# Attention output products placed inside the HGRN turns, token-wise norm roots, and an eight-tile first part of the expert values

## What is computed

```python
# HGRN2, per head, in chunks of tokens; then norm and gate
A = einsum('bthd,btshd,bshd->bhts', qc, decay, kc)
o = einsum('bhts,bshv->bthv', A, vc) + einsum('bthd,bhdv->bthv', qc * exp(b), S)
S = exp(bl)[..., None] * S + einsum('bshd,bshv->bhdv', kc * exp(bl[:, None] - b), vc)
o = rmsnorm(o, g_hgrn) * silu(hg)
# merge: each mixer's output is projected to 1024 channels and gated by channel
mix = sigmoid(za) * (attn @ w_a) + sigmoid(zb) * (o @ w_b)
x = x + mix @ w_out
# experts: every token takes a few of 16,384; e runs over a token's experts
x = x + sum_e gate[e] * gelu(h @ u[e]) * v[e]
```

## Time and profile before

| | us |
|---|---|
| median of 3 runs | 2248.57 (2244.8 to 2250.56) |
| profiled run | 2249.61 |
| its span | 2248.0 |
| PE busy | 2088.7 (93%) |
| DVE busy | 1338.3 (60%) |
| POOL busy | 555.1 (25%) |
| ACT busy | 360.5 (16%) |
| mean granted clock of TensorE | 0.943 |

### The profile page before, as it was taken

The page is one execution under the profiler, slowest core; times in us unless marked ns, Lnnn a source line. Parts: engine busy times, 40 slices in busy tenths (PEclk is TensorE's granted clock), DMA queues, the critical chain, the costliest instruction groups (busy, mean ns, idle before and its releaser), DMA issues. The chain is left out here.

```text
span 2248.0 us, 24729 instructions
## 1 busy us (share of the span) xinstructions
PE 2088.7 (93%) x8839; PEld 1568.6 (70%) x8839; DVE 1338.3 (60%) x2881; ACT 360.5 (16%) x745; POOL 555.1 (25%) x516
## 2 busy tenths in 40 slices
PE   6968989976999999899999999999699999999997
PEld 4755577753889966677777777777477777777776
DVE  2005377763454158599999999988635455455233
ACT  1001137641010111211111222221000000000011
POOL 1001100013000000233335555554434244343000
PEclk9988999987559999999999999999899999999998
DMA  3142221113232332487889999999999999999421
GB/s 131 38 68 76 75 94 50 45 37 114 94 133 81 113 113 94 162 298 274 291 324 362 403 402 396 399 401 408 399 381 339 376 369 383 387 353 356 181 80 62
DMA packets 168033, 513.81 MB, mean 229 GB/s; under 512 B 18422, under 2 KB 52862, under 8 KB 164327
## 3 DMA queue, kind: packets, MB, share of 16 engines
q1 hardware_dynamic: 93782, 273.61, 33.6%
q0 software_dynamic: 60288, 213.96, 24.9%
q10 hardware_dynamic: 13840, 24.66, 2.9%
HBM read 462.42 MB, written 49.74 MB: 228 GB/s over the span
## 5 line engine op out<-in xcount | busy, mean ns | idle before, releaser
L1938 PE MATMUL ex_ps<-proj,ex_ring 128*128 128x320 f32 x2048 | 558.3, 436 | 20.5 <-DMA ex_ring<-in_v 20.5
L1883 PE MATMUL ex_ps<-h,ex_ring 128*128 128x320 f32 x2048 | 566.0, 433 | 5.9 <-DMA ex_ring<-in_uT 5.9
L1938 PEld LDWEIGHTS ex_ps<-proj,ex_ring 128*128 128x128 f32 x2048 | 392.4, 192 | 186.0 <-DMA ex_ring<-in_v 21.7
L1883 PEld LDWEIGHTS ex_ps<-h,ex_ring 128*128 128x128 f32 x2048 | 384.2, 191 | 156.6 <-DMA ex_ring<-in_uT 6.1
L2114 DVE TENSOR_TENSOR proj<-proj 128x320 f32<-128x320 f32 x124 | 53.0, 490 | 253.9 <-DMA proj<-scratch_a 234.4
L2048 DVE SCALAR_TENSOR_TENSOR gx_sum<-proj,gx_sum 128x1024 f32<-128x1024 f32 x120 | 154.2, 1285 | 9.2 <-DVE gx_sum L2048 0.9
L2030 DVE CUSTOM_DVE_ANT_0 proj<-proj,gx_tokens 128x1024 f32<-128x1024 f32 x120 | 143.9, 1222 | 2.1 <-DMA proj<-in_u,at_last 1.8
L1785 POOL DMA_INDIRECT scores<-in_u,at_last x26 | 30.9, 1187 | 435.6 <-POOLq L1504 389.1
L1791 POOL DMA_INDIRECT proj<-in_v,at_last x76 | 105.3, 1386 | 84.0 <-DVE gx_sum L2048 68.2
L379 PE MATMUL gate_ps<-h,work 128*128 128x260 f32 x512 | 120.5, 389 | 3.4 <-DMA work<-in_w_t 3.4
L1785 POOL DMA_INDIRECT proj<-in_u,at_last x76 | 88.2, 1161 | 141.9 <-DVE proj L2030 129.5
(11 more groups left out here) (387 smaller groups left out, 2743.1 us busy)
## 6 DMA issues: line engine op xcount, KB each, us to landing
ex_ring<-in_uT SPq DMA_DIRECT2D x128, 512.0 KB, 6.7
ex_ring<-in_v SPq DMA_DIRECT2D x128, 512.0 KB, 6.9
scratch_a<-ex_gelu ACTq DMA_DIRECT2D x64, 320.0 KB, 7.1
scratch_w<-proj SPq DMA_DIRECT2D x10, 2048.0 KB, 12.0
proj<-scratch_a SPq DMA_DIRECT2D x15, 1280.0 KB, 10.0
proj<-scratch_w SPq DMA_DIRECT2D x15, 1280.0 KB, 11.2
work<-in_w_t SPq DMA_DIRECT2D x37, 512.0 KB, 3.6
mg_ring<-in_w_q SPq DMA_DIRECT2D x32, 512.0 KB, 3.4
```

The lines of the kernel that those rows point to most:

```text
L1883: last = nc.tensor.matmul(y[:, bank(n), 0:TD], u[:, n % UR, k, :], xn[:, k, 0:TD], start=(k == 0), stop=(k == DC - 1))
L1938: last = nc.tensor.matmul(y[:, m, 0:TD], ring[:, (E1 + e) % UR, m * P:(m + 1) * P], hidden_of(part_of[e])[:, e - parts[part_of[e]][0], :], ...
```

## The change

**HGRN and merge.** The 64 attention products move out of `merge_tail` into `hgrn`, as sixteen half products (`att_product(i)`: one of eight output tiles m, one half of 260 tokens, four products each). Each turn holds four: after the scores, after the second chunk of kv, in the middle of `out` (at h == 2), and after `sample_out(2t)`. Each waits for its weights (even i) and for the gate of the one before (`s_eg`), since all share one half bank. DVE's `gate_att(i)` multiplies in place into `proj` (ZA). The weights (eight loads of 256 KB on ACT's queue, between the rows of v) take two of the four `spare` buffers, so the rows of v have two left. `out(t)` has one bank now, and waits for the copy of out(t - 1). In `merge_tail` only the second half of w_ab is loaded; the norm's sums are made token-wise, as twenty one-column products into one bank, so one root and one reciprocal of 128x20 do for all heads, and PE spreads them again over partitions by products with the identity (four of 128 columns and one of 8 for each head). DVE reads the spread root from PSUM, and `mix` is the sum of `proj` (ZA) and the gated HGRN product.

```diff
+        wa = [t.rearrange("p (k n) -> p k n", k=4) for t in spare[2:4]]
+        vb = spare[0:2]
+        WR = len(wa)
+        per_turn = DC * 2 // NT
...
+                def att_product(i):
+                    m = i // 2
+                    if i % 2 == 0:
+                        pe.wait_ge(s_wa[m % WR], 16 * (m // WR + 1))
+                    if i >= 1:
+                        pe.wait_ge(s_eg, i)
+                    o, c0, c1 = att_at(i)
+                    for k in range(4):
+                        last = nc.tensor.matmul(o, wa[m % WR][:, k, :], attT[:, k, c0:c1], start=(k == 0), stop=(k == 3))
+                    last.then_inc(s_ea, 1)
...
                     pe.wait_ge(s_st, (4 * t + 3) * HG)
-                    if t >= 2:
-                        pe.wait_ge(s_oc, t - 1)
+                    if t >= 1:
+                        pe.wait_ge(s_oc, t)
                     for h in range(HG):
-                        o = pO[:, t % 2, h * P:(h + 1) * P]
+                        if h == HG // 2:
+                            att_product(t * per_turn + 2)
+                        o = pO[:, 0, h * P:(h + 1) * P]
...
                 for t in range(NT):
+                    i = t * per_turn
                     scores(t)
+                    att_product(i)
                     for j in range(P // CH):
                         kv_of(t * (P // CH) + j)
+                        if j == 1:
+                            att_product(i + 1)
                     if t >= 1:
                         sample_out(2 * t - 1)
                     out(t)
                     sample_out(2 * t)
+                    att_product(i + 3)
...
+                def gate_att(i):
+                    dve.wait_ge(s_ea, i + 1)
+                    o, c0, c1 = att_at(i)
+                    gate = proj[:, ZA + i // 2, c0:c1]
+                    nc.vector.tensor_tensor(gate, o, gate, ALU.mult).then_inc(s_eg, 1)
...
+                load_weights(0)
+                load_weights(1)
+                act.wait_ge(s_vd, 16)
+                load_row(0)
+                load_row(1)
+                for t in range(1, NT):
+                    load_weights(2 * t)
+                    load_row(2 * t)
+                    load_row(2 * t + 1)
+                    load_weights(2 * t + 1)
...
+            act.wait_ge(s_ms, 1)
+            nc.scalar.activation(tiny[:, 0, :], ps[:, 7, 0:HG * (NT + 1)], ACT.Sqrt, scale=1.0 / P,
+                                 bias=c.eps[:, 0:1]).then_inc(s_rt, 1)
...
-                if hd >= 2:
-                    pe.wait_ge(s_rt, hd - 1)
-                for j in range(2):
-                    last = nc.tensor.matmul(ps[:, 4 + 2 * (hd % 2) + j, 0:HALF], c.ones[:, :],
-                                            sq[:, hd, j * HALF:(j + 1) * HALF], start=True, stop=True)
-                last.then_inc(s_ms, 1)
-            for m in range(DC):
-                if m % 2 == 0:
-                    pe.wait_ge(s_ab[m // 2], 16)
-                if m >= 2:
-                    pe.wait_ge(s_ga, m - 1)
-                for j in range(2):
-                    for k in range(4):
-                        last = nc.tensor.matmul(ps[:, 2 * (m % 2) + j, 0:HALF], ab[:, m, k, :],
-                                                attT[:, k, j * HALF:(j + 1) * HALF], start=(k == 0), stop=(k == 3))
-                last.then_inc(s_p, 1)
+                for t, n0 in enumerate(starts):
+                    i = hd * (NT + 1) + t
+                    last = nc.tensor.matmul(ps[:, 7, i:i + 1], sq[:, hd, n0:n0 + P], c.ones[:, 0:1], start=True, stop=True)
+            last.then_inc(s_ms, 1)
+            pe.wait_ge(s_iv, 1)
+            for hd in range(HG):
+                out = root_of(hd)
+                for t in range(NT + 1):
+                    col = tiny[:, 1, hd * (NT + 1) + t:hd * (NT + 1) + t + 1].to_broadcast([P, P])
+                    if t < NT:
+                        nc.tensor.matmul(out[:, t * P:(t + 1) * P], col, c.ident[:, :], start=True, stop=True)
+                    else:
+                        last = nc.tensor.matmul(out[:, TP:N], col, c.ident[:, P - TS:P], start=True, stop=True)
+                last.then_inc(s_sp, 1)
...
-            pe.wait_ge(s_n, 4 * HG)
+            pe.wait_ge(s_n, 3 * HG)
...
-                dve.wait_ge(s_rt, hd + 1)
-                link(nc.vector.reciprocal(rt[:, hd, :], rt[:, hd, :]))
+                dve.wait_ge(s_sp, hd + 1)
                 link(nc.vector.scalar_tensor_tensor(out=hgoT[:, hd, :], in0=hgoT[:, hd, :],
-                                                    scalar=c.small["g_hgrn"][:, 0:1], in1=rt[:, hd, :],
+                                                    scalar=c.small["g_hgrn"][:, 0:1], in1=root_of(hd)[:, 0:N],
                                                     op0=ALU.mult, op1=ALU.mult))
                 link(nc.vector.tensor_tensor(hgoT[:, hd, :], hgoT[:, hd, :], proj[:, HGT + hd, :], ALU.mult))
...
+            dve.wait_ge(s_rt, 1)
+            nc.vector.reciprocal(tiny[:, 1, :], tiny[:, 0, :]).then_inc(s_iv, 1)
+            for hd in range(HG):
                 norm(hd)
-                gate_att(2 * hd - 2)
-                gate_att(2 * hd - 1)
-            for hd in range(HG):
                 dve.wait_ge(s_sg, hd + 1)
                 link(nc.vector.tensor_tensor(hgoT[:, hd, :], hgoT[:, hd, :], sg[:, hd, :], ALU.mult))
-            gate_att(DC - 2)
-            gate_att(DC - 1)
```

```diff
-    HEAD = 4
+    HEAD = 8
+    QUAD = 4
...
-                return small[:, HEAD * TD:HEAD * TD + LATE * HEAD * WB].rearrange("p (k e n) -> p k e n", k=LATE, e=HEAD)
+                t = M.S_full[0].rearrange("p g k -> p (g k)")
+                return t[:, 0:LATE * HEAD * WB].rearrange("p (k e n) -> p k e n", k=LATE, e=HEAD)
...
-            for r in range(2):
-                sp.wait_ge(s_as[r], 16 * (E1 // 4))
-            for r in range(2):
-                sp.wait_ge(s_ws[r], 16 * (NWB // 2))
-            sp.wait_ge(s_h, HEAD)
-            load_hidden(1)
-            load_weights(1)
-            load_weights(2)
             for e in range(E1):
                 if e + UR < E1:
                     sp.wait_ge(s_pv, e + 1)
                     load_v(e + UR)
+                if e == 2:
+                    for r in range(2):
+                        sp.wait_ge(s_as[r], 16 * (E1 // 4))
+                        sp.wait_ge(s_ws[r], 16 * (NWB // 2))
+                    sp.wait_ge(s_h, HEAD)
+                    load_weights(1)
+                    load_hidden(1)
+                    load_weights(2)
...
+                if (quad + 1) * QUAD < HEAD:
+                    continue
+                while chunk < U_CHUNKS + (NC - U_CHUNKS) * (quad + 1) // (E1 // QUAD):
```

More of the change, by code:

```diff
@@ L994, in hgrn, with att_at @@
         s_m = a.sem("hg_zero_state")
-        VR = len(spare)
+        s_wa = [a.sem(f"hg_att_weights_loaded{r}") for r in range(WR)]
+        s_ea, s_eg = (a.sem("hg_" + x) for x in ("att_product", "att_gated"))
+        def att_at(i):
+            j = i % 2
+            return pO[:, 1, 0:HALF], j * HALF, (j + 1) * HALF
+        VR = len(vb)
         s_vd = a.sem("hg_v_rows_stored")
@@ L1099, in _ @@
                     ins.then_inc(s_sc, 1)
+                    i = t * per_turn
+                    gate_att(i)
                     for j in range(P // CH):
@@ L1117, in _, with load_weights, load_row @@
                 dve.wait_ge(s_oc, NT + 1)
+                dve.wait_ge(s_eg, DC * 2)
             @block.scalar
             def _(act):
[L1121 to L1123 removed]
+                def load_weights(m):
+                    if m >= WR:
+                        act.wait_ge(s_ea, 2 * (m - WR + 1))
+                    act.dma_start(wa[m % WR], I["w_ab"][m, :, 0:4, :]).then_inc(s_wa[m % WR], 16)
+                def load_row(b):
                     if b >= VR:
                         act.wait_ge(s_vc, b - VR + 1)
[L1126 removed]
+                    act.dma_start(vb[b % VR], v_dram[b:b + 1, :].to_broadcast([P, HG * P])).then_inc(s_vl[b % VR], 16)
+                act.dma_start(v_dram, hitok[0:TS, NT, :]).then_inc(s_vd, 16)
+                load_weights(0)
[8 more added lines that the diff above has]
+                    load_weights(2 * t + 1)
             @block.sync
@@ L1305, in merge_tail, with root_of @@
         a = Alloc(nc, ctx)
-        ab = M.S_all[:, 0:DC * DC * P].rearrange("p (m c n) -> p m c n", m=DC, c=DC)
+        wb = M.S_all[:, 0:DC * 4 * P].rearrange("p (m c n) -> p m c n", m=DC, c=4)
         mix, tb = M.mix, a.sb("mg_b", [P, 2, TD])
         ps = a.ps("mg_ps", [P, DC, 512])
-        s_ab = [a.sem(f"mg_weights_loaded{i}") for i in range(4)]
-        s_p, s_q, s_ga, s_gb, s_m = (a.sem("mg_" + k) for k in (
-            "att_product", "hgrn_product", "att_gated", "hgrn_gated", "mixed"))
+        s_wb = [a.sem(f"mg_weights_loaded{i}") for i in range(4)]
+        s_q, s_gb, s_m = (a.sem("mg_" + k) for k in ("hgrn_product", "hgrn_gated", "mixed"))
```

(26 more changed lines are left out.)

34 lines of the change are left out of this document (11 added, 23 removed).

## The result

The changed kernel takes 2254.43 us (median of 14 runs, 2251.0 to 2260.77) against 2248.32 us (14 runs) before: ratio 1.0029, 95% interval 1.0022 to 1.0037. By the medians that is 6.1 us slower. The profiled execution of the changed kernel took 2260.77 us, the longest of its 14, so 6 us of what its trace shows are its own; the first experiment says where they lie.

The account below looks back on a forecast made before the run. TensorE, busy for 93% of the span, was taken as the bound, with a low clock in HGRN and stalls in v. 2249.6 + 20 - 12 - 0.4 = 2257.2, less 1.0, gave 2256 us, own range 2247 to 2265.

Parts of the forecast that it names:

- its own yardstick of 6.7 us: Whole kernel: about 0.3%, what a measurement tells from no change; "same" runs from 2242 to 2255 us.
- HGRN, +20: HGRN: sixteen added half products at a changing clock, +17.5, and a weights' wait, +2.5; range -9 to +59 us.
- the clock's rise: HGRN: dense products across each turn's seam lift the clock at the scores' end; a turn takes 24.9 us.
- The terms that I put at nothing: HGRN: waits for DVE's gates, for the single bank of out and for broadcast rows in two buffers, each 0 us.
- Rival A: HGRN: the clock never rises, +59 us, with merge -9: 2298 us; chance 0.07.
- rival B: HGRN: the clock stays up throughout, -9 us, with merge -19: 2220 us; chance 0.10.
- Merge, -12: Merge tail: first HGRN product 14.2 us earlier, with 2 us given back for slower products.
- v, -0.4: v part: later start 5.8 and waits of 5 and 7 us against old stalls of 18.2; range -15.3 to +12.
- the 9 us of tile 7: v part: upper bound of the wait for tile 7, with loads landing in 25.5 us; 5 was taken.
- the 12 of tile 13: v part: upper bound of the wait for tile 13, with a tile's median 6.9 us after 21.5; 7 was taken.
- the -9 of HGRN at 1.00: HGRN: lower bound of its term, all products at the upper clock, 72 us of work and "10 less".
- Rival C: v part: waits for tiles 7 and 13 vanish, only a later start of 2.9 us is left, 2241 us; chance 0.16.

Follow-up runs that it names:

- the first experiment: Two kernels, each with one half of the change, the rest as before: HGRN and merge alone 2250.63 us (ratio 1.0007), experts alone 2252.02 us (1.0014).
- the evenly spread kernel: Changed kernel with the same 64 products, alternating banks and sixteen spread over each turn without a dense run: 2286.36 us, ratio 1.0176 to before.
- the second table: Changed kernel with the same 64 products, alternating banks, a dense start and a more careful spread of places: 2236.03 us, ratio 0.9957 to before.

## Why the prediction was right

It said 2256 and slower by a little, for these reasons; 2254.4 was measured. By its own yardstick of 6.7 us the 6.1 us lie at the upper edge of "same"; with 14 runs of each kernel the interval, 1.0022 to 1.0037, is clear of no change. That the sum came within 2 us is in part luck: by the means of the traces HGRN cost 6 us less than forecast (+14 for +20), while v and the u part cost +4.2 where -0.4 stood.

**HGRN, +20: right in kind, near in size, with the clock's rise at the wrong place.** +18.2 in the profiled execution, +14 in the mean of four traces. The weights' wait is 2.62 us where I had worked out 2.5, and the mean clock 0.71 where I had said near 0.7. The terms that I put at nothing held: for the gates, the one bank and the rows in two buffers PE waits 0.29 us in all. The clock goes up and down as I had said, and three of its four falls lie in `out`. The step that failed is the rise: I put it at the end of the scores behind each seam, and three of five rises came in `out`, behind its half product, while the first turn had none until there and stayed at 0.50 for 27.65 us. The two errors have opposite signs, so the length of a turn came out better than its picture. I had also not seen that the changes come at other places from one execution to the next (first rise at 600.1 in one trace, at 580.3 in another), with 92.6 to 101.6 us for the same code; what decides between them isn't shown. Rival A, 57 us from a clock that stays low, came true for three turns of four in the evenly spread kernel, and rival B in the second table: both were states of the same products; between the two kernels their order made the difference, though within the even spread one order stood at both levels. The Trainium skill, "TensorE: Matmul & The Clock Gate", section "Why this matters for your kernels", says that a TensorE kept busy gets its full clock; the trace doesn't agree, with 110.40 busy us of 110.40 at 0.50.

**Merge, -12: right in size, with another engine at its end.** -14.1 to the first HGRN product and +2.8 for the products, -11.3. The sums took 8.70 us (I had 9.2), then comes a reciprocal of 0.28. Behind it I had let PE's spread set the pace, 2.34 us a head; in the trace PE was through with it at 691.7, the clock at 1.00 from 689 to 692, and DVE's three multiplications a head, 2.25 us from 687.82 to 690.07, set it. Both give the same stretch, 11.4 us measured and 11.5 worked out.

**v, -0.4: the direction of two terms right, one mis-sized.** The start came 3.3 us later, not 5.8; tile 7 waited 5.63 us (I took 5); tile 13 waited 11.41, where I took 7 and named 12 as the end. The step that was mis-sized is the landing of the weights load ahead of it, 25.6 us and not 21.5. In all v and its start are +2.8 to +3.5. Some bounds were added up loosely: by my own terms the 9 us of tile 7 are 8.3, the 12 of tile 13 are 11.2, the -9 of HGRN at 1.00 is -10, and the 0.37 for "same" is 0.355; none moves the sum. Rival C, waits that vanish, was the wrong case for the kernel as it is, and the right mechanism in reverse: the small pieces do lose one for one to the gathers, and without these the waits go. The Trainium skill, "DMA: Bandwidth & Descriptors", section "Queues, rings and completion order", has whole packets of some 9 to 17 descriptors drained from a queue in turn; 1765 packets of q0 beside 1837 of q1 don't decide in what groups they went, but no gain for the small pieces is to be seen in 25.6 us. That they would lose less was my own inference: groups of equal number from both queues would come out one for one as well.

**Not priced:** +1.4 us in the u part. In each trace with the changed HGRN, u's first tile waits 6.9 to 7.3 us for its load and not 5.9, and takes 7.2 to 7.4 us and not 6.3. One instruction fetch stands in the DMA queues there that isn't in the traces without that change; that it delays the load was not tried.

## What to carry to other kernels

Where PE is busy and its granted clock low, ask first in what order its products stand: the same products cost 130 us or 78 by their order, and added work in the right places made the stage 5 us shorter than without it (78.4 against 83.4). When a load that waits is cut into small pieces, look at what else is in the DMA queues; moving the other traffic to a stretch with room was worth more than asking for the load sooner. And take the length of a stage whose clock changes from several executions, not from one.

## What the runs showed of the hardware

- With PE busy all the time, the granted clock stayed at 0.50 for 110 us of products of which a part contract 32 rows or move one column, and at 1.00 for 75.00 us of the same products in another order, with PE busy 73.30 us of these.
- The level depended on what came ahead: in one execution a turn in the same order took 36.7 us at 0.50 twice and 21.8 us once the clock had risen behind its scores; the same records had not raised it at the two seams before.
- The same code changed level at other places from one execution to the next: four traces of one HGRN took 92.6, 97.5, 97.7 and 101.6 us.
- A load of 1,280 KB in 1 KB pieces took 12.1 us beside few gathers and 25.6 us beside many, with packets moved one for one.
